# First-layer attention of a two-block transformer kernel: values stationary, merge and gate kept in feature order

## What is computed

```
qkv, gate = split(rmsnorm(x) @ w_in)            # w_in: 1024 x 10240
for g, (window, dil) in enumerate(groups):      # three groups, 16 heads of 64 each
    s = q_g @ k_g.T / 8, masked to the window
    m = max(s);  p = exp(s - m);  den = sum(p)
    out_g = (p @ v_g) / den;  lse_g = m + log(den)
alpha = softmax([lse_g over g]);  o = sum(alpha_g * out_g)
y = (o * silu(gate)) @ w_out
h = x + rmsnorm(y)
```

## Time and profile before

| | |
|---|---|
| median of three runs | 2751.18 us (2751.0 to 2754.81) |
| the profiled execution: its own time | 2750.86 us |
| its span | 2749.3 us |
| TensorE busy, matmuls | 2693.3 us (98%), 13721 instructions |
| VectorE, ScalarE, GpSimd busy | 1222.0, 1049.7, 1139.1 us |
| granted TensorE clock, mean | 0.997 of full speed |

### The profile page before, as it was taken

How to read it: one execution, slowest core, us unless ns; L and a number is a source line. 1 busy time by engine, 2 the same in 40 slices (tenths; PEclk the granted TensorE clock), 3 DMA queues, 4 the chain that set the end, 5 groups by cost and what they waited for, 6 DMA issues and landing times.

```text
span 2749.3 us, 36052 instructions
## 1 busy us (share of the span) xinstructions
PE 2693.3 (98%) x13721; PEld 2154.6 (78%) x13721; DVE 1222.0 (44%) x2467; ACT 1049.7 (38%) x2005; POOL 1139.1 (41%) x894
## 2 busy tenths in 40 slices
PE   8999999999999999999999999999999999999998
PEld 6887878888778877766788888887777678888887
DVE  4434343443555356544236424265644424642425
ACT  3333434353345344353333424233445333342422
POOL 4434343434432443333364444444333336444442
PEclk9999999999999999999999999999999999999999
DMA  5424343432431242224252333324223425233331
GB/s 188 135 85 140 95 127 96 122 119 75 126 92 55 75 124 78 77 89 130 93 175 83 115 99 93 92 82 125 83 70 88 134 92 182 73 120 95 92 98 56
DMA packets 214912, 286.39 MB, mean 104 GB/s; under 512 B 16846, under 2 KB 154546, under 8 KB 213972
## 3 DMA queue, kind: packets, MB, share of 16 engines
q1 hardware_dynamic: 214740, 284.08, 34.0%
HBM read 248.31 MB, written 18.94 MB: 97 GB/s over the span
## 4 chain that ended last, share of the span: by engine, by line
PE 94%; DVE 3%; ACT 1%; issue 1%; POOL 0%; DMA 0%; DVEq 0%; ACTq 0%; POOLq 0%
PE banks L1663 38%; PE banks L1660 29%; PE banks L1656 13%; PE banks L1793 2%; PE banks L1681 2%; PE banks L1775 1%; PE banks L1720 1%; PE banks L1879 1%; PE banks L1696 1%; PE banks L1814 1%; PE banks L1902 1%; PE banks L1952 1%; PE banks L1865 1%; PE banks L1760 1%; PE banks L1836 1%
## 5 line engine op out<-in xcount | busy, mean ns | idle before, releaser
L2962 POOL TENSOR_TENSOR WS<-WR,WS 128x512 fp32r<-128x512 f32 (+2 forms) x676 | 855.3, 1298 | 1067.2 <-ACT WS L2015 1067.2
L1663 PE MATMUL banks<-WS,UT 128*128 128x512 f32 (+1 forms) x3696 | 798.5, 366 | 4.5 <-DVE UT L2373 4.5
L1663 PEld LDWEIGHTS banks<-WS,UT 128*128 128x128 f32 x3696 | 605.9, 190 | 134.4 <-issue 37.4
L1660 PE MATMUL banks<-UT,WS 128*128 128x512 f32 (+1 forms) x2832 | 660.7, 392 | 0.7 <-ACT AR L2202 0.7
L1660 PEld LDWEIGHTS banks<-UT,WS 128*128 128x128 f32 (+1 forms) x2832 | 526.0, 187 | 125.5 <-issue 15.8
L2015 ACT ACTIVATE WS<-WR 128x1024 fp32r<-128x1024 f32 (+1 forms) x344 | 333.0, 1018 | 223.5 <-PE banks L1663 153.6
L1656 PE MATMUL banks<-UT,WS 128*128 128x512 f32 x1536 | 372.6, 396 | 0.0
L1656 PEld LDWEIGHTS banks<-UT,WS 128*128 128x128 f32 x1536 | 282.2, 188 | 64.6 <-issue 6.2
L1663 PE MATMUL banks<-WS,AT 128*128 128x512 f32 x1296 | 308.2, 396 | 0.0
L2960 POOL TENSOR_TENSOR WS<-WR,WS 128x512 fp32r<-128x512 f32 x128 | 181.0, 1445 | 259.9 <-ACT WS L2011 259.9
L1663 PEld LDWEIGHTS banks<-WS,AT 128*128 128x128 f32 x1296 | 242.5, 188 | 58.5 <-ACT WS L2015 0.7
(11 more groups left out here) (225 smaller groups left out, 2676.8 us busy)
## 6 DMA issues: line engine op xcount, KB each, us to landing
WR<-in_w_in SPq DMA_DIRECT2D x112, 512.0 KB, 3.6
WR<-in_w_up SPq DMA_DIRECT2D x88, 512.0 KB, 3.5
WR<-in_dil_w_in SPq DMA_DIRECT2D x64, 512.0 KB, 3.9
WR<-in_w_down SPq DMA_DIRECT2D x40, 512.0 KB, 3.7
WR<-in_diff_w_in SPq DMA_DIRECT2D x32, 512.0 KB, 3.8
WR<-in_dil_w_in SPq DMA_DIRECT2D x32, 256.0 KB, 3.2
AR<-AF SPq DMA_DIRECT2D x128, 64.0 KB, 2.4
AR<-AF SPq DMA_DIRECT2D x64, 128.0 KB, 2.5
```

The source lines that it names most:

```text
L1660: mm = pe.matmul(B[bank][0:c, :], w[part][:, kk, g * P:g * P + c], act[:, other, kk, :], start=start, stop=stop)
L1663: mm = pe.matmul(B[bank][:, off:off + n], act[:, other, before_k + kk, g * P:g * P + P], w[part][:, kk, :], start=start, stop=stop)
L2962: ge.tensor_tensor(slot(i, 1)[:, s], raw(i)[:, s], slot(i, 0)[:, s].bitcast(F32), ALU.subtract).then_inc(lo_p.sem, 1)
```

## The change

- **Sums.** `out1` has the values stationary (128x64, one head) and moves the 128 turned weights; the two heads write partitions 0-63 and 64-127 of one bank, alternately. The result is features x tokens. ScalarE copies it to `XT` (far) or `N0` (near) in feature order.
- **Merge.** Only the maxima and sums (4 floats a token) go through `near`. `weigh1` stands alone; then `share1` (VectorE, small operations) 2 ticks later, `rows1` (TensorE turns the 128x16 shares, ScalarE copies 16x128) 5 ticks, `send1` (DMA, 8 KB to DRAM) 7, `fetch1` (two DMAs that read the rows back, each row to 64 partitions, 512 KB together) 9, and `merge1` in three parts (VectorE, one 128x512 operation each) 12, 13 and 14 ticks later.
- **Gates.** `gates_by_features`: the four tiles are feature-major, 48 matmuls of 512 columns. `gate1`, `times1` and `parts1` replace `gate`, `times` and `chunk`; no transposes. `parts1` makes the high part (ScalarE) and low part (VectorE) from `XT`, with the reordering of tokens.
- **Order.** R_G1 1.38 becomes 1.7. The attention has one `yield` less per head pair. For l1k23 `rotate` comes 1 tick later instead of 3 and `spread` 4 instead of 5; the last far units are released after 8 ticks instead of 9. `parts1` of chunks 4 to 7 stands in the opening of l1o.

Cut to its core:

```diff
-R_G1 = 1.38
+R_G1 = 1.7
+    def gates_by_features(self, merged, late):
+        for j in range(4):
+            while j < 3 and 2 * j + 1 not in merged:
+                self.tick()
+                yield 1
+            def deal(i, t, j=j):
+                self.step("gate1", i, t)
+                if 2 * j + t not in merged:
+                    late[2 * j + t] = (i, t, j)
+                else:
+                    self.step("times1", i, t, j)
+                    if j < 2:
+                        self.soon(4, lambda: self.step("parts1", 2 * j + t))
+            yield from self.feature_major(f"l1g{j}", deal)
...
                     self.step("weigh1", p)
-                    yield
-                    self.step("merge1", p)
-                    merged.add(p)
+                    for due, name in ((2, "share1"), (5, "rows1"), (7, "send1"), (9, "fetch1")):
+                        self.soon(due, lambda name=name: self.step(name, p))
+                    for part in range(3):
+                        self.soon(12 + part, lambda part=part: merge(p, part))
                     yield
...
+        while 6 not in merged:
+            self.pend.pop(0)[1]()
         self.step("reload", "l1o")
...
+        opening = [(0, 0, 4), (1, 0, 4), (2, 0, 2), (3, 0, 2), (2, 2, 4), (3, 2, 4)]
+        for n, c in zip((0, 2, 5, 7), range(4, 8)):
+            opening.insert(n, (parts, c))
...
-                    for hh in range(2):
-                        r = 64 * hh
-                        for j in range(w // P):
+                    for j in range(w // P):
+                        for hh in range(2):
+                            r = 64 * hh
...
-                            mm = pe.matmul(B[ob][:, r:r + 64], fat(7168 + 512 * e + 256 * hh + j * P, P), vj,
+                            mm = pe.matmul(B[ob][r:r + 64, 0:P], vj, fat(7168 + 512 * e + 256 * hh + j * P, P),
                                            start=(j == 0), stop=(j == w // P - 1))
+                elif kind == "rows1":
+                    p, = a
+                    pe.wait_ge(shared.sem, shared.at[p])
+                    pe.transpose(B[k][0:16, 0:P], SM[:, QT + 16:QT + 32], IDN).then_inc(rows_turned.sem, 1)
...
+                    if part == 0:
+                        ve.wait_ge(sums_out.sem, sums_out.at["1", l1_last(p, 1)])
+                        ve.wait_ge(rows_in, 32 * (p + 1))
+                        tt(y, y, s0, ALU.mult).then_inc(near_shared.sem, 1)
+                    elif part == 1:
+                        tt(x, x, s1, ALU.mult).then_inc(far_shared.sem, 1)
+                    else:
+                        tt(x, x, y, ALU.add).then_inc(merged.sem, 1)
...
+                elif kind == "send1":
+                    sy.wait_ge(rows_out.sem, rows_out.at[p])
+                    sy.dma_start(share_rows[p], turned_shares[0:16, :]).then_inc(rows_sent, 16)
+                elif kind == "fetch1":
+                    sy.wait_ge(rows_sent, 16 * (p + 1))
+                    rows_of = share_rows[p].rearrange("(g r h) l -> h g r l", g=2, h=2)
+                    for h in range(2):
+                        sy.dma_start(shares_of(p)[64 * h:64 * h + 64].rearrange("p g (r l) -> p g r l", r=4),
+                                     rows_of[h].unsqueeze(0).to_broadcast([64, 2, 4, P])).then_inc(rows_in, 16)
```

187 lines of the change are left out of this document (133 added, 54 removed).

## The result

The changed kernel takes 2757.99 us in the median of 19 runs (2756.23 to 2758.88), the kernel before 2751.33 (2749.32 to 2757.87, 19 runs on the same chip): ratio 1.0021 [1.0015, 1.0027]. It is slower by 0.2%, where 2743.2 was forecast. The profiled execution has a span of 2757.6 us against 2749.3, +8.3.

The account below looks back on a forecast made before the run. TensorE, with matmuls for 98% of the span, was taken to bound the kernel. Savings of 16.8 us less costs of 8.8 gave net -8.0, forecasting a median of 2743.2 us, range 2733 to 2754.

Parts of the forecast that it names:

- Step 1: First layer's value matmuls with values stationary: saves 7.1 us, bounds 18.6 saved to 4.4 lost.
- Steps 2 to 4: Feature-major gates save 2.1 us; no chunk transposes saves 3.5, 2.7 and 1.4 in waits; turning shares adds 0.9.
- steps 2 and 3: Feature-major gates save 2.1 us; dropping chunk transposes saves 3.5, two TensorE waits 2.7, waits for far scores 1.4.
- step 5: Denser attention beside the gate tiles, 1.7 steps a tick: adds 1.7 us of waits, bounds 0 and 5.
- step 3: Chunk transposes dropped: saves 3.5 us, two TensorE waits of 2.7, and 1.4 of waits for far scores.
- Step 6: End of the attention: TensorE waits 6.2 us for the last pair's shares, fetched behind the reload; 1.9 to 8.3.
- rival B: At the attention's end the fetch isn't held up by the reload: wait 1.9 us, total 2738.9; chance 0.20.
- C: Value matmuls in column halves gain nothing, costs in front and behind eating it: 2754.7 us; chance 0.10.
- D: `merge1` waiting for fetched shares holds VectorE's queue, then TensorE, at all eight pairs: 2759 us; chance 0.11.
- E: Attention beside the gates runs ahead of ScalarE (5 us) and end wait is 8.3: 2748.6 us; chance 0.13.
- list of signs: Trace signs, among them one TensorE wait of about 6 us before the third l1o tile's second half; wrong under 3 or over 9.

Follow-up runs that it names:

- b1: Kernel before with only the new value matmuls (values stationary), output not the reference's: 2743.95 us, ratio 0.9972.
- a2: Changed kernel without the send and fetch of the last head pair's shares, output not the reference's: 2758.19 us, ratio 1.0024.
- c1: Changed kernel with every `fetch1` issued at 8 ticks instead of 9: 2756.92 us, ratio 1.0011.
- e3: Changed kernel without the send and fetch of shares for pairs 6 and 7, output not the reference's: 2756.64 us, ratio 1.0015.
- g1: Changed kernel with low parts of chunks 4 to 7 reading a PSUM bank instead of SBUF, output not the reference's: 2755.18 us, ratio 1.0012.
- a4: Changed kernel with 24 matmuls of the second token block pulled forward into the opening of l1o: 2751.21 us, ratio 0.9991.
- e1: c3 without the 24 matmuls pulled forward: 2752.93 us, ratio 1.0002.
- c3: Changed kernel joining a4, c1 and c2, with the third l1o tile's high part not waiting for pair 6's merge: 2746.73 us, ratio 0.9976.
- f1: c3 with the shares' turn and send one tick sooner, fetch and merges two ticks sooner: 2744.90 us, ratio 0.9975.
- a1: Changed kernel with the 3 MB reload issued ahead of the last pair's send and fetch: 2760.31 us, ratio 1.0036.
- c2: Changed kernel with `parts1` of chunks 4 and 5 among the gate tiles and an own place for pair 6's shares: 2758.42 us, ratio 1.0017.
- d3: Changed kernel with 24 unread matmuls ahead of each of the two waiting l1o pieces: 2756.04 us, ratio 1.0014.
- d2: Kernel before with only R_G1 raised from 1.38 to 1.7: 2756.90 us, ratio 1.0016.
- g2: Kernel before with low parts of chunks 4 to 7 reading SBUF instead of the PSUM bank, output not the reference's: 2754.11 us, ratio 1.0009.

## Why the prediction was wrong

**Step 1, values stationary: right.** Eight and what they cost behind come to 0.59 + 0.18 to 0.22, the 0.77 named; 8.2 us in b1 for 7.1, and 33.2 us on the value line for about 36. The 64-column load takes 136 ns in the new line too. The rule of the Trainium skill that column tiling disables fast weight load made no difference here. I had overlooked that its page TensorE: Matmul & The Clock Gate (Weight-path perf modes) says fast weight load isn't used for FP32 at all; these are f32 rows, so by that page there was nothing to lose; no run here shows a fast load to compare with.

**Steps 2 to 4: the structure right, the gain not seen.** The line of the chunk transposes, L1788 in the new kernel's numbering, doesn't stand before 858 us, the gate groups of twelve take 2.77 to 2.97 but for one, a turn of the shares 0.27 in the timeline. The first stretch is 6.5 us shorter (b1's 5.6), so the small steps do no harm there. But in the second stretch b1, with step 1 alone, has 125.2 us (474.63 to 599.87) and the kernel after 127.5. By my terms steps 2 and 3 take 2.1, 2.2 (the transposes of five of the eight chunks lie there) and 1.5 off: 119.4. What ate them is step 5.

**Step 5, the denser attention: mis-sized.** I put 1.7 with a bound of 5. It cost 127.5 - 119.4 = 8.1 in the profiled execution. The trace shows where: TensorE's waits from 470 to 600 us are 7.8 us, b1's 4.2 of which 1.8 is the wait that step 3 removed, so 5.4 are new; and behind the longest, 1.81 for an exponential, the clock fell:

```profile
552.51 0.66 PE L1834 MATMUL banks<-CT,AF 128*128 128x128 f32 x4 [1.81 <-ACT AF L2165]
552.92 4.59 PE L1719 MATMUL banks<-UT,WS 128*128 128x512 f32 x12
```

4.59 for twelve against 3.02, 1.6 us more. That is 7.0 of the 8.1. But the 1.6 differs from execution to execution. The runs a2, c1, e3, g1, a4, e1, c3 and f1 have the same wait in the same place and kept the clock, as here in a4, while a1, c2 and d3 lost it as the kernel after did:

```profile
553.89 0.66 PE L1841 MATMUL banks<-CT,AF 128*128 128x128 f32 x4 [1.82 <-ACT AF L2172]
554.30 3.00 PE L1726 MATMUL banks<-UT,WS 128*128 128x512 f32 x12
```

Their second stretch is 125.9 to 126.1 us, that of the other four 127.5. So the step costs 6.5 us with a kept clock and 8.1 without, over the bound of 5 both times. The step counted places where a turn and its product touch; what it left out is that ScalarE's exponentials stand behind 2 us of weight split (the chain has `ACT WS L2082`, 1.99, just ahead of them), and that a wait can cost clock. d2 confirms the kind of cost: the pace alone takes 4.5 in the kernel before.

**Step 6, the end: the step that failed.** Forecast 6.2 (1.9 to 8.3), found 13.6 + 3.6 = 17.2. My chain was followed through one pair's data, counted from the end of the last value matmuls (590.1):

| | forecast | found |
|---|---|---|
| shares turned | +8.3 | +8.2 |
| reload issued | +9.3 | +9.2 |
| 8 KB landed | +11.8 | +14.0 |
| fetch landed | +20.3 | +24.7 |
| chunk 7's low part ready | +25.6 | +35.0 |

The first two rows are right, and the fetch did stand behind the reload (9.7 to 10.0 us), so rival B is out. Put ahead of the reload it landed in 4.0 (c1). The Trainium skill's rule of ring order (DMA: Bandwidth & Descriptors, Queues, rings and completion order) agrees with that. But this is the part that mattered least: with no trips at all only 1.7 of the 14.5 went (e3), as long as the rest of the order stood. The sum lacked three things. First, the rest of the queues: I costed copies, merges, multiplies and parts at nothing because they were as many as before, but merge 7, which was alone before, now stands in one file with the low parts of chunks 5 and 6, and chunk 5, which I thought early, is held through ScalarE by pair 6's merge. Second, the price of an operation: merges 0.69 and low parts 1.10 by the earlier trace rows, found 1.49 to 2.15 while GpSimd splits the weights (last section). Of this I had "strided operands double" in the bound of 8.3; operands matter (1.08 for 0.69 at 605.19, GpSimd idle), but GpSimd doubles on top. Third, the clock, 3.6. A part of the second is the change's own doing, costed at nothing: low parts read SBUF now, which g1 puts at 1.3 us and g2 at 2.5. The causes are shown to act; their shares of the 17.2 do not add up from single runs, because each link that c1, c2, e3 or g1 removes uncovers the next.

Steps 5 and 6 put 6.4 and 11.0 more on than the sum had for them; step 1 took 1.1 more off. That is the 16.3 by which the span (+8.3) missed the forecast's -8.0, though each was sized in one execution.

One number of step 6 came true by luck. The wait before the third l1o tile's second half, the one that I named, is 6.07 us, for 6.2. TensorE reached that place at +29.1, not at +19.4, since it had stood 7.5 us before the first half and ran at a lower clock behind it, and the low part came at +35.0, not at +25.6: two errors of some 10 us that cancel.

**The rivals.** C (halves buy nothing) is refuted by b1. D (VectorE held in mid-stage) is out: TensorE has no new wait for VectorE in the projection stretch, only the 1.0 and 0.5 beside the gates. E (dense attention 5, end wait 8.3) had both right places and both sizes too small. D's 2759 lies near the measured 2757.99, but for a reason that the trace doesn't have. No rival had the mechanism that did it, a helper's queue at the end. My list of signs said one wait of about 6 us and there were two, 13.6 together; but its limits, under 3 or over 9 for the named wait, didn't catch this, since that wait alone was 6.07. A limit should have stood on the sum of TensorE's waits in the stage.

## What to carry to other kernels

Where a stage ends and a queue of another begins, write down the whole queue of each helper engine there with its times, not only the chain of the datum that is last; an operation "as many as before" is not free when it comes later and stands with others. Take durations of an operation from a stretch in which the neighbours run that will run there, and with its operands where they will lie. A pace is a cost too: test it alone, in the old kernel, before it is built into a new one; and if a wait at a stage's end cannot be taken away, independent matmuls in that place gave more (a4, 8 us) than any one cut of the chain did (c1, c2, e3, g1: at most 1.7 in the end stage). And look at the same place in several executions before a slower stretch is put down to an edit: the clock alone moved one by 1.6 us.

## What the runs showed of the hardware

**VectorE and GpSimd.** A low part of 128x512 on VectorE took 1.07 us at 624.01 and 2.07 to 2.15 at 612 to 620, merges 1.08 and 1.49 to 2.13. GpSimd's timeline of the kernel after, 600 to 630 us:

```profile
607.49 5.85 POOL L3079 TENSOR_TENSOR EX<-WR,EX 128x512 fp32r<-128x512 f32 x4 [9.37 <-ACT EX L2082]
613.30 7.83 POOL L3079 TENSOR_TENSOR WS<-WR,WS 128x512 fp32r<-128x512 f32 x4
```

All long ones begin within 607.5 to 621.1. The kernel before splits the same tiles there in 5.65 and 5.07, and its low part from a bank took 1.10 beside them. g1 and g2 show what decides: a low part with both inputs in SBUF takes up to twice its time beside GpSimd (1.56 to 2.15), or keeps its time (1.17) while the piece of GpSimd that it meets takes 2.12 in place of 1.28; one with an input in PSUM stays at 1.06 to 1.12. The Trainium skill (SBUF — State Buffer, SBUF: two separate sides) says that a VectorE operation with two SBUF inputs and a GpSimd operation that reads SBUF take one port pair in turn, each for its whole length. The runs agree: the longest times, 2.20 on VectorE (e3) and 2.17 on GpSimd (g2), stay within the two times alone together (1.07 and 1.27). The prediction should have weighed this rule.

**The clock behind a wait.** Six matmuls took 2.90 us behind waits of 2.94 (d3) and of 4.75 to 11.2, and 1.60 to 1.68 behind 0.97, 1.34, 2.27 and, once, 3.04 (f1). The windows 612 to 616 and 624 to 628 us of the kernel after read PEclk 0.50, which is 1.2 GHz. Since 2.94 and 3.04 fell on either side, the length of the wait alone doesn't decide. Nor did it among the gate tiles, where the same wait of 1.81 to 1.82 us was followed by 4.52 to 4.59 for twelve matmuls in five runs and by 3.00 to 3.02 in eight. What else decides, no run here shows.

**Small transfers.** The 8 KB of shares landed after 3.3 us in the median of the run, and after 5.2 with weights and, 0.4 us behind it, the reload in flight; in a1, behind the 3 MB, after 9.9. The 256 KB read back landed in 4.2 in the median, and behind the 3 MB in 9.7 to 10.0.
